# Moving modulation rows between stages, and seven-product pairs from the sixth pair on, in a transformer block in fp32

## The reference

```python
o = rms_norm(o, head_norm_g) * (1.0 - lam_0)
o = o.reshape(b, s, BRANCH) * jax.nn.silu(z)
x = x + o @ w_out                                            # attention's end
mod = (silu(c) @ ada_w + ada_b).reshape(B, 3, 3, D)          # 72 columns of 128
shift, scale, gate = mod[:, :, 0], mod[:, :, 1], mod[:, :, 2]
h = modulate(rms_norm_2(x, norm_g[0]), shift[:, 0], scale[:, 0])
x = x + 0.5 * gate[:, 0] * swiglu(h, ffn1_w_in, ffn1_w_out)  # first feed-forward
h = modulate(rms_norm_2(x, norm_g[1]), shift[:, 1], scale[:, 1])
x = x + gate[:, 1] * token_mixer(h, ...)                     # mixer
h = modulate(rms_norm_2(x, norm_g[2]), shift[:, 2], scale[:, 2])
x = x + 0.5 * gate[:, 2] * swiglu(h, ffn2_w_in, ffn2_w_out)  # second feed-forward
return rms_norm_2(x, final_g)
```

## Time and profile before

| what | value |
|---|---|
| median of 3 runs | 1809.32 us (1809.29 to 1809.45) |
| profiled execution | 1809.3 us, its span 1807.1 us |
| TensorE busy | 1782.5 us, 99% of the span |
| VectorE busy | 1252.1 us, 69% |
| ScalarE busy | 946.8 us, 52% |
| GpSimd busy | 141.7 us, 8% |

### The profile page before, as it was taken

How to read it: one execution, slowest core, us unless ns; L and a number is a source line. 1 busy time by engine, 2 the same in 40 slices (tenths; PEclk the granted TensorE clock), 3 DMA queues, 4 the chain that set the end, 5 groups by cost and what they waited for, 6 DMA issues and landing times.

```text
span 1807.1 us, 24794 instructions
## 1 busy us (share of the span) xinstructions
PE 1782.5 (99%) x9644; PEld 1472.2 (81%) x9644; DVE 1252.1 (69%) x2164; ACT 946.8 (52%) x1631; POOL 141.7 (8%) x161
## 2 busy tenths in 40 slices
PE   8999999999999999999999999999999999999998
PEld 6777777777888788998886877788888878999887
DVE  6777877776536778886559778745664779888533
ACT  5777777777423424565225766344432444656521
POOL 2100000000011110000100020100100200000010
PEclk9999999999999999999999999999999999999999
DMA  5432332332253572334534223310552423333331
GB/s 194 140 105 82 117 105 70 117 94 94 71 175 105 188 280 83 104 104 158 168 120 141 81 81 100 98 55 24 205 203 93 143 79 94 107 105 103 110 98 64
DMA packets 59780, 210.44 MB, mean 116 GB/s; under 512 B 6736, under 2 KB 9168, under 8 KB 59024
## 3 DMA queue, kind: packets, MB, share of 16 engines
q1 hardware_dynamic: 47248, 164.54, 28.1%
q0 software_dynamic: 12416, 44.31, 7.5%
HBM read 203.58 MB, written 5.25 MB: 116 GB/s over the span
## 4 chain that ended last, share of the span: by engine, by line
PE 92%; DVE 4%; ACT 2%; issue 1%; DMA 0%; SPq 0%; DVEq 0%; ACTq 0%
PE ps L1513 20%; PE ps L1516 19%; PE ps L1514 19%; PE ps L1548 5%; PE ps L1549 5%; PE ps L1551 5%; PE ps L1631 2%; PE ps L1655 2%; PE ps L1592 2%; PE ps L1593 2%; PE ps L1599 1%; PE ps L1684 1%; ACT wH L2353 1%; DVE wL L1844 1%; PE ps L1643 1%
## 5 line engine op out<-in xcount | busy, mean ns | idle before, releaser
L1844 DVE TENSOR_TENSOR wL<-wr,wH 128x1024 fp32r<-128x1024 f32 (+2 forms) x325 | 348.5, 1075 | 222.7 <-ACT wH L2353 222.0
L2353 ACT ACTIVATE wH<-wr 128x1024 fp32r<-128x1024 f32 (+2 forms) x325 | 301.4, 930 | 261.9 <-PE ps L1516 231.3
L1513 PE MATMUL ps<-hH,wH 128*128 128x512 f32 (+1 forms) x1000 | 403.3, 403 | 1.1 <-DVE hL L2011 1.0
L1516 PE MATMUL ps<-hH,wL 128*128 128x512 f32 (+1 forms) x1000 | 391.1, 391 | 1.0 <-DVE wL L1844 0.7
L1514 PE MATMUL ps<-hL,wH 128*128 128x512 f32 (+1 forms) x1000 | 389.6, 390 | 0.0
L1513 PEld LDWEIGHTS ps<-hH,wH 128*128 128x128 f32 (+1 forms) x1000 | 187.3, 187 | 53.4 <-issue 13.1
L1516 PEld LDWEIGHTS ps<-hH,wL 128*128 128x128 f32 (+1 forms) x1000 | 186.9, 187 | 44.9 <-DVE wL L1844 4.0
L1514 PEld LDWEIGHTS ps<-hL,wH 128*128 128x128 f32 (+1 forms) x1000 | 187.3, 187 | 38.2 <-issue 2.6
L1513 PE MATMUL ps<-gffn,wH 128*128 128x512 f32 (+1 forms) x422 | 160.8, 381 | 0.2 <-DVE xT L2125 0.2
L1514 PE MATMUL ps<-gffn,wH 128*128 128x512 f32 (+1 forms) x422 | 159.6, 378 | 0.0
L1516 PE MATMUL ps<-gffn,wL 128*128 128x512 f32 (+1 forms) x422 | 159.5, 378 | 0.0
(11 more groups left out here) (364 smaller groups left out, 3374.9 us busy)
## 6 DMA issues: line engine op xcount, KB each, us to landing
wr<-wst SPq DMA_DIRECT2D x280, 512.0 KB, 3.5
vffn<-wfd POOLq DMA_DIRECT2D x24, 512.0 KB, 5.7
fed<-wfd POOLq DMA_DIRECT2D x20, 512.0 KB, 3.8
xT<-wfd POOLq DMA_DIRECT2D x16, 512.0 KB, 4.3
wr<-wst SPq DMA_DIRECT2D x16, 384.0 KB, 3.0
affn<-wfd POOLq DMA_DIRECT2D x12, 512.0 KB, 4.7
xT<-xin SPq DMA_DIRECT2D x8, 256.0 KB, 7.1
xT<-xin SPq DMA_DIRECT2D x2, 1024.0 KB, 5.9
```

The costliest lines, as they stand in the source:

```text
L1513: e.matmul(o, hi, vh, start=k == 0, stop=False)
L1516: i = e.matmul(o, lo, vh, start=False, stop=k == t.nk - 1)
L1844: e.tensor_tensor(dst, x, hi.bitcast(F32), ALU.subtract).then_inc(s[name], 1)
L2353: e.activation(dst, x, ACT.Copy).then_inc(s[name], 1)
```

## The change

`SEVEN` becomes (5, 5). The first stage of rows ends at 24 in place of 16: rows 16 to 23 run at step 5 of the z tiles of heads 6 to 13, and `mod` makes the first gate as well. The stage in the plain pairs, with `fed_later`, is gone. The output tiles of the first feed-forward take rows 24 to 47, up to four per tile, with two buffers (places of sg, ac and tmp of affn; the sum of squares moves to rs), `mod2` stands in tile 4 and the `raw` steps of the mixer in tiles 5 to 7. The mixer's tail takes rows 48 to 71, every 3.5 steps.

```diff
--- before.py
+++ after.py
@@ -117,11 +117,14 @@
 
 
 NFED = 72
-FED_FIRST = 16
-FED_LAST = 40
-FED_ENDS = (FED_FIRST, FED_LAST, 52, NFED)
-FED_BUFS = (3, 4, 1, 2)
-SEVEN = (11, 5)
+FED_FIRST = 24
+FED_MIX = 40
+FED_LAST = 48
+FED_ENDS = (FED_FIRST, FED_LAST, NFED)
+FED_BUFS = (3, 2, 2)
+FED_STEPS = [(0, 13), (0, 20)] + [(c, k) for c in range(1, 6) for k in (3, 9, 14, 20)] + [(6, 3), (6, 9)]
+RAW_STEPS = {(5, 5): (0, 1), (5, 11): (2,), (6, 5): (3, 4), (6, 11): (5,), (7, 5): (6,)}
+SEVEN = (5, 5)
 
 
 def norm_count(n):
@@ -237,14 +240,6 @@
         stage = sum(i >= end for end in FED_ENDS)
         later = i + FED_BUFS[stage]
         self.add("fed", i=i, next=later if later < FED_ENDS[stage] else None, fed=self.sig("fed"))
-
-    def fed_later(self, i, k):
-
-        if i < 12 and k == 3:
-            for j in range(2):
-                self.fed(FED_FIRST + 2 * i + j)
-        if k == 7 and i == 12:
-            self.add("mod2")
 
     def raw(self, n, c):
 
@@ -612,7 +607,8 @@
             i, _ = zr.take()
             d = dict(h=h, i=i, free=z_free[i], zs=sig("zs"), zm=sig("zm"), gh=sig("gh"), gl=sig("gl"), on=self.on[h])
             z_free[i] = ("gl", d["gl"])
-            self.whole(Tile("z", src("l0_w_in", 6144 + 128 * h), self.pb01.take()[1], "h", ("zs", d["zs"]), n=0, d=d))
+            self.whole(Tile("z", src("l0_w_in", 6144 + 128 * h), self.pb01.take()[1], "h", ("zs", d["zs"]), n=0, d=d),
+                       (lambda: self.fed(10 + h)) if h < 14 else None)
             if h < 12:
                 add("fold", h=h - 6, ze=h - 5, gh=sig("gh"), gl=sig("gl"))
         self.h_lasts[1] = len(self.slots)
@@ -678,14 +674,17 @@
             for k in self.steps_of(t):
                 if c == 0 and k < 22 - 11:
                     self.a_split(f, k + 11)
-                if n == 1 and (c, k) == (0, 14):
-                    add("fed_start", stage=2, after=("fu", 22), i=FED_LAST, n=FED_BUFS[2])
-                if n == 1 and 0 < c < 7 and k in (9, 20):
-                    self.fed(FED_LAST + 2 * (c - 1) + k // 20)
+                if n == 1 and (c, k) == (0, 5):
+                    add("fed_start", stage=1, after=("fu", 22), i=FED_FIRST, n=FED_BUFS[1])
+                if n == 1 and (c, k) in FED_STEPS:
+                    self.fed(FED_FIRST + FED_STEPS.index((c, k)))
+                if n == 1 and (c, k) == (4, 12):
+                    add("mod2")
+                if n == 1 and (c, k) in RAW_STEPS:
+                    for i in RAW_STEPS[c, k]:
+                        self.raw(2, i)
                 if k == 5 and c > 0:
                     square(c - 1)
-                    if n == 1:
-                        self.raw(2, c - 1)
                 if n == 3 and k == 14 and c > 0:
                     add("final_g", c=c - 1, nsq=self.count["nsq"])
                 if n == 1 and c == 7 and k in (2, 9):
@@ -727,14 +726,10 @@
         for i, at in ((1, 13), (2, 22)):
             turn.setdefault(at, []).insert(0, (t_hi, i))
         self.whole(up(1))
-        if f == 0:
-            add("fed_start", stage=1, done=raw_done, i=FED_FIRST, n=FED_BUFS[1])
         at = -16 * (begin - 5)
         for j in range(2, begin):
-            for i, t in enumerate((gate(j), up(j))):
-                for k in self.steps_of(t):
-                    if f == 0:
-                        self.fed_later(2 * (j - 2) + i, k)
+            for t in (gate(j), up(j)):
+                for _ in self.steps_of(t):
                     for fn, *a in turn.get(at, ()):
                         fn(*a)
                     at += 1
@@ -1095,10 +1090,10 @@
         B = clock[0]
         for h, step in zip(range(DNH), range(11, 75, 8)):
             at(B + step, zd_out, h)
-        add("fed_start", stage=3, after=("hn", 8), i=FED_ENDS[2], n=FED_BUFS[3])
-        for i in range(FED_ENDS[2], NFED):
-            at(B + 4 + 4 * (i - FED_ENDS[2]), self.fed, i)
-        at(B + 4 + 4 * (NFED - FED_ENDS[2]), lambda: add("mod3"))
+        add("fed_start", stage=2, after=("hn", 8), i=FED_LAST, n=FED_BUFS[2])
+        for i in range(FED_LAST, NFED):
+            at(B + 4 + 7 * (i - FED_LAST) // 2, self.fed, i)
+        at(B + 4 + 7 * (NFED - FED_LAST) // 2, lambda: add("mod3"))
         pb6 = Ring([0, 1, 2, 3, 4, 5])
         for h in range(DNH):
             run(zd(h, pb6))
@@ -1241,11 +1236,9 @@
             aH = [parts[c] for c in (42, 43, 38, 39, 40, 41)] + parts[t0:t0 + 16]
             t_at = {2: 0, 1: 1, 3: 2, 4: 3}
             tH, tL = ({i: G.t[:, 512 * t0 + 2048 * t_at[i] + a:512 * t0 + 2048 * t_at[i] + a + 1024] for i in t_at} for a in (0, 1024))
-            if f == 0:
-                late_row, late_buf = V[:, 0:1024], [V[:, 1024 + 1024 * i:2048 + 1024 * i] for i in range(FED_BUFS[1])]
             A = Arena(F, f"affn{f}", 4992)
             if f == 0:
-                ff0_row, ff0_buf = A.t[:, 2560:3584], A.t[:, 3584:4608]
+                late_row, late_buf = A.t[:, 2560:3584], [A.t[:, 3584:4608], A.t[:, 1536:2560]]
             ff.append(dict(aH=aH, aL=aL, av=av, tH=tH, tL=tL, s_sum=[c5(V, c) for c in range(38, 42)],
                            t_tmp=[V[:, 16384 + 1024 * i:17408 + 1024 * i] for i in range(3)], sq=A.several(2), rs=A(), tmp=A.several(2), sg=A.several(2),
                            ac=A.several(2), row=A(384)))
@@ -1298,9 +1291,7 @@
                 return xT[:, at:at + 1024], xT[:, 0:1024]
             if i < FED_LAST:
                 return late_buf[i % FED_BUFS[1]], late_row
-            if i < FED_ENDS[2]:
-                return ff0_buf, ff0_row
-            return mix_buf[i % FED_BUFS[3]], mix_row
+            return mix_buf[i % FED_BUFS[2]], mix_row
 
         s = {name: ctx.enter_context(nc.semaphore("s_" + name)) for name in plan.count}
         for name in ("small", "const", "first", "lam", "hi", "lo", "slot", "th", "rowd", "xb0", "xb1", "csb", "mod", "modd", "saved", "bd", "ba",
@@ -1341,7 +1332,7 @@
 
         def square_sum(n):
 
-            return {0: WT[:, 0:512], 1: acc1, 2: ff[0]["tmp"][0], 3: tq[0], 4: ff[1]["tmp"][0]}[n]
+            return {0: WT[:, 0:512], 1: acc1, 2: ff[0]["rs"], 3: tq[0], 4: ff[1]["tmp"][0]}[n]
 
         def norm_views(n):
 
@@ -2100,6 +2091,7 @@
                     w.wait_ge(s["fed"], FED_FIRST)
                     e.tensor_tensor(mod[:, 0:FED_FIRST], mod[:, 0:FED_FIRST], S("ada_b", 0, FED_FIRST), ALU.add).then_inc(s["mod"], 1)
                     w.wait_ge(s["mod"], 1)
+                    own(e.tensor_scalar(gate[:, 0:8], mod[:, 16:24], 0.5, None, ALU.mult, ALU.bypass))
                     factors(range(1))
                 elif what == "fed":
                     i = d["i"]
@@ -2109,11 +2101,11 @@
                     e.tensor_tensor_reduce(out=buf, in0=buf, in1=c_row, scale=1.0, scalar=0.0, op0=ALU.mult, op1=ALU.add,
                                            accum_out=mod[:, i:i + 1]).then_inc(s["fed"], 1)
                 elif what in ("mod2", "mod3"):
-                    a, b = (FED_FIRST, FED_LAST) if what == "mod2" else (FED_LAST, NFED)
+                    a, b = (FED_FIRST, FED_MIX) if what == "mod2" else (FED_MIX, NFED)
                     w.wait_ge(s["fed"], b)
                     e.tensor_tensor(mod[:, a:b], mod[:, a:b], S("ada_b", a, b), ALU.add).then_inc(s["mod"], 1)
                     w.wait_ge(s["mod"], 2 if what == "mod2" else 3)
-                    for sub in (0,) if what == "mod2" else (1, 2):
+                    for sub in () if what == "mod2" else (1, 2):
                         own(e.tensor_scalar(gate[:, 8 * sub:8 * sub + 8], mod[:, 24 * sub + 16:24 * sub + 24], 0.5, None,
                                             ALU.mult, ALU.bypass))
                     factors((1,) if what == "mod2" else (2,))
@@ -2745,8 +2737,6 @@
                         e.dma_start(modd[0:1024].rearrange("(p n) -> p n", n=8), csil).then_inc(s["rowd"], 16)
                         w.wait_ge(s["rowd"], 16)
                         w.wait_ge(s["nl"], d["nl"])
-                    elif d["stage"] == 1:
-                        w.wait_ge(s["slot"], d["done"])
                     else:
                         w.wait_ge(s[d["after"][0]], d["after"][1])
                     e.dma_start(c_row, modd[0:1024].unsqueeze(0).broadcast_to([128, 1024])).then_inc(s["csb"], 16)
```

## The result

| | before | after |
|---|---|---|
| median (lowest to highest), us | 1809.38 (1809.07 to 1809.92) | 1815.03 (1814.50 to 1815.96) |
| profiled execution, its span | 1809.3, 1807.1 | 1814.97, 1812.9 |

Six runs each. The ratio is 1.0031 (95% interval 1.0021 to 1.0041): the changed kernel is 5.65 us slower, 0.3%. The forecast was 1811.3, the range 1806.0 to 1815.5, and "no change that can be told" was the likeliest. The time lies in the range, but on the side of the rival called slower, whose own figure was 1813.1 to 1817.1.

The account below looks back on a forecast made before the run. The prediction took TensorE's row of matmuls, busy 99% of the span, to bound the kernel. From 1809.3 us, -3.32 (pairs) + 0 + 0 (moved rows) + 5.35 (tail stall) gave 1811.3 us, range 1806.0 to 1815.5.

Parts of the forecast that it names:

- no change that can be told: Whole kernel: time within about 0.2% (3.6 us) of before, chance 0.65.
- the rival called slower: Mixer's tail: transfers held up more often than before, stall 7.1 to 11.1 us, 1813.1 to 1817.1 us; chance 0.25.
- Part 1: First feed-forward: six more seven-product pairs shorten TensorE's row of matmuls, gain 3.32 us, bounds 3.3 and 4.9.
- the gaps of the transition: At the first seven-product pair: TensorE gaps of 2.9 us in the second feed-forward, 1.4 in the first.
- Parts 2 and 3: Eight rows in the z tiles, 24 instead of 12 in the first feed-forward's output tiles: cost 0 each.
- the walk: Mixer's tail: VectorE's list of work followed in order with times from the old profile; it gave a 5.35 us stall.
- the cycle of a pair in part 3: First feed-forward's output tiles: reduction, GpSimd wake and transfer take 5.4 to 6.9 us, against rows due every 7.48 us.
- Part 4: Mixer's tail: 24 rows every 3.5 steps instead of 20 every 4 make TensorE stall 5.35 us.
- those 4.4 us and the others 3.83: Mixer's tail: assumed transfer times, 4.4 us for rows issued up to 2.2 us behind a split, 3.83 for the rest.
- the case that I named as likeliest: Mixer's tail: stall of 4 to 7 us, total 1809.9 to 1813 us, chance 0.55.

Follow-up runs that it names:

- e5: After, with four rows more (28) in the first feed-forward's output tiles and 20 in the mixer's tail, every four steps: 1806.05 us, ratio 0.9983.
- e9: After, with a third buffer for the tail's rows and SEVEN = (11, 5): 1810.00 us, ratio 1.0007.
- e2: Before, with four rows moved from the first feed-forward's output tiles into the tail and the new pace there: 1818.53 us, ratio 1.0052.
- e4: After, with the tail's 24 rows every four steps and what reads them 12 steps later: 1806.84 us, ratio 0.9988.
- e1: After, with the first feed-forward's seven-product pairs from place 11 again, SEVEN = (11, 5): 1820.42 us, ratio 1.0061.
- e8: After run once more, unchanged, as a second look at the profile: 1815.20 us, ratio 1.0040 against before.

## Why the prediction came out as it did

**Part 1, the pairs: right, 3.00 against 3.32.** That the first feed-forward would come out as the second was the right way to read its transition. The 0.3 lies at the first seven-product pair, in the timeline of TensorE of after:

```profile
643.89 0.39 PE L1539 MATMUL ps<-gffn,wH 128*128 128x256 f32 x1 [0.90 <-ACT affn L2381]
```

The second feed-forward has 0.53 at the same place in its own order, 0.37 less. What makes ScalarE later in the first is not settled. The prediction put the gaps of the transition to VectorE's sums; the row names ScalarE, and two more gaps of 0.76 us behind it have no releaser. The price was right, that cause isn't shown.

**Parts 2 and 3, rows in the z and output tiles: nothing, as forecast.** No gap in either stretch; VectorE at 39.73 and 86.56 us, where the walk had 40.2 and 88. e5 and e9 show the same through the times. (Two slips in the prediction's sums have no weight: the cycle of a pair in part 3 adds up to 5.3 to 6.8, not 5.4 to 6.9, and a stall of 4 us to 1810.0, not 1809.9.)

**Part 4, the tail: the mechanism was right, the size was not, 9.74 against 5.35.** Two things were missed, and the rows tell them apart.

First, the walk is right up to the eleventh tile. Its lag was 1.2 us at the eighth, 2.0 at the tenth and 5.3 at the eleventh tile; the gaps add up to 1.8 there, then 2.2, then 5.0. After that the walk had the lag stay, and the trace has a fourth gap of 2.51. The step that failed is the transfer's time: "I gave those 4.4 us and the others 3.83". Two rows of which VectorE works off one directly behind the other are issued again 1.2 us apart, and the split that stands next brings a weight load. Of three such transfers together one took 6.6 us. Before, the longest that VectorE waited for was 5.76. With 4.4 the row of 1325.84 would have been there at 1330.2, and its split, 2.2 us sooner, would have left some 0.3 of that gap. The times that I took from the old rows didn't contain the state that the new pace makes: once VectorE is behind, its rows come in pairs. The trace of before had that state, outside the rows that VectorE waited for. These are the landings of all 20 old rows, where the prediction says "3.8 to 5.8" (the 6.2 is the second of the first two, issued together), and those of the plain pairs, two rows per tile, from the list of transfers (size, median):

```profile
DMA to landing us min/median/max: 3.8/3.8/6.2
```

```profile
vffn<-wfd POOLq DMA_DIRECT2D x24, 512.0 KB, 5.7
```

The rival called slower is this, and the time lies inside its figure. The condition that I gave for it, a mean transfer over 4.2 us, tells little: behind the first two rows the mean from issue to landing is 4.2 in after and 4.1 in before. It is a few long ones, each with a split behind it, that cost. My objection to it, that a stalled TensorE spaces the weight loads out, holds for the mean (233 GB/s in the tail against 241 before) and didn't keep those few apart.

One of the causes of that pairing is a late issue: at 1318.37 GpSimd issues 0.96 us later than the 0.37 behind the reduction, with nothing that the profile shows to wait for. The row lands late (1323.07), the next is there at once (1324.31), and the pair is made. All profiles of after and its variants have one such issue in the tail, before and e2 have none. As e2 loses 9.2 us without it, it isn't needed for the loss; and e4 and e5 have it and no gap, so it isn't enough either.

Second, the half clock behind the fourth gap, 1.8 us. The forecast counted a gap at its own length only.

**The sum.** -3.32 + 5.35 became -3.00 + 9.74, and 0.93 of the run's own start lowered it. The forecast missed by 3.7 us and so named the wrong case as likeliest. The range held by 0.5 us, since its upper end had been drawn from the slower rival; for the case that I named as likeliest (1809.9 to 1813) that is luck.

**What was to show it.** 222 us with 1428 matmuls of 256 columns: 222.38. No gaps in z and output tiles: so. Gaps in the eighth to eleventh tile, "5 us in sum, and the last reduction some 9 us later than 1335.4": eighth to twelfth, 7.5 us, and 1343.24, which is 11.8 us later when both are counted from the tail's start.

## What to carry to other kernels

A buffer that an engine in strict order empties, and that is issued again only then, has a cycle of its own: here 1.15 (reduction) + 0.37 + 3.5 to 6.6 us of transfer, over two buffers 2.5 to 4.1 us a row. A pace of 3.5 steps = 2.38 us is below all of it; one of four steps, 2.72, with 4.5 us of slack at the start, was not too quick in the profiles of before, e4 and e5. Price such a move with the transfer times of the crowded state that it makes, not with the old rows' mean, and look for spare room for one more buffer first: it was worth 8.4 us here. And take the parts of a change apart: three of its four parts gained 3.3 us together (e5), the fourth alone lost 9.2 (e2).

## What the hardware showed that was not expected

**The clock falls behind a short gap, not always.** In after, e1 and e8 the granted clock was 0.50 (the 1.2 GHz level) for two to four us at a gap of 2.35, 2.94 and 2.65 us: in after it fell 0.9 us behind the first matmul after the gap, in e1 and e8 0.4 us ahead of it; it stayed at 1.00 behind 2.46 and 2.54 in e2, 2.92 in e9, and behind the third gap of after, 2.68. What decides it is open: the length of the last gap doesn't.

**Transfers of a size differ by almost two.** A row of 512 KB in the tail landed in 3.5 us at the shortest and 6.6 at the longest in after (7.0 in e1), 8.6 with three buffers (e9). The Trainium skill (DMA: Bandwidth & Descriptors, Issuing engines are not separate DMA queues) says that transfers of all issuing engines interleave on the same 16 engines; the rows of 6.3 and 6.6 us in after stand where two rows and a weight load of SyncE are under way together, and around the second the DMA share is 0.83 to 1.01 in every microsecond from 1327 to 1333, which agrees. The first two rows of the tail, 5.3 and 6.0 us, are under way with each other and the transfer of c.
